# Feed-forward products in runs: all of a weight unit's 512-column products, then all of its 256-column ones

## The chip, the cores and the metric

The kernel runs on one core of one Trainium2 chip. The metric is the device time of one execution in microseconds. A profile of one execution gives, for each instruction, its engine, its source line, its start and its duration.

## What is computed

Two blocks of two layers each, on one sequence of 256 tokens with 1024 channels, all in float32. Each layer is a mixer and then a feed-forward stage with a residual. The mixers are a causal attention with rotary positions, a latent attention, a pooling mixer and an attention with a bias table. The four feed-forward stages have one form (2816 inner channels, a causal convolution of width 3 along the tokens, gelu in the first block and silu in the second):

```
g = xn @ w_gate
gc = conv_b + sum(conv_w[j] * shifted(g, 2 - j) for j in range(3))
h = act(gc) * (xn @ w_up)
x = x + h @ w_down
```

## The kernel before

**Splitting.** A float32 product is made of reduced-precision passes. A weight w is split into a high part `whi` and a low part `wlo = w - whi`; an activation x into `xx[:, k, 0, :]` (high) and `xx[:, k, 1, :]` (low). The products high*high, low(x)*high(w) and high(x)*low(w) are kept. Tokens are the columns that move through TensorE, 256 of them; the weight block of 128x128 is what is loaded before a product. With the high weight block loaded, both parts of x pass in one product of 512 columns (line 463); with the low weight block loaded, only the high part of x passes, 256 columns (line 465), added to the first 256 columns of the same PSUM bank. One 512 and one 256 product on one block are called a pair here. `block_wide` issues a pair; `across_wide` issues the pairs of the two output blocks m = 0 and 1 of one contraction block k, into the two banks of the PSUM tile it is given. So the order of TensorE was 512, 256, 512, 256, and so on, with a new weight block before every product. Where 512 columns are not used, `three` issues three products of equal width (lines 422 to 424).

**Weight units.** Weights come in units of up to 128x2048 elements, 180 in all, in the order of use. SyncE loads unit n into one of 3 `raw` buffers. ScalarE copies it, rounded, to one of 5 `whi` buffers (`hi(n)`, signalled by `s_hi`); VectorE subtracts to get `wlo` (`lo(n)`, signalled by `s_lo`, which also frees `raw`). TensorE waits on `s_lo` (`weights_here`) or `s_hi` (`high_here`), and its last product on a unit raises `s_used`, which frees the unit's ring place and tells ScalarE and VectorE that the bank is complete.

**A feed-forward stage** (`ffn(s)`, s is F0, F1, F2 or F3) has 34 units: eleven pairs of a gate unit and an up unit (each 8 k blocks by 2 output blocks), then twelve down units (four output groups c, each of 8, 8 and 6 k blocks over the 22 blocks of the hidden activation `hx`). The first gate and up units are interleaved block by block because the input blocks arrive one at a time. Gate and up results go to the PSUM tiles `banks0`, `banks1`, `TB` and `SB` in turn; `s_gr` and `s_ub` say that a tile has been read. ScalarE and VectorE make the convolution, the activation and the two parts of `hx` (`s_hl` counts finished blocks). For c = 0 TensorE waits on `s_hl` before each k, for c = 3 `last_pair` runs the block m = 0 in pairs and the block m = 1 with `three`.

**Other callers.** `across_wide` also serves `project`, the last two output units of each of the three attention mixers. Each engine runs its own list in a fixed order, written by hand; there is no planner.

In the profile, line numbers are those of the kernel file. Lines 679, 680 and 686 are products of 512 columns in the attention mixers (`high` and `low` in `heads_mixer`), where activations are the loaded block and weights move. Lines 518 and 519 are the two products that spread the sums of squares.

Of the kernel before, what the change touches and what calls it, by code (L numbers as in the profile page):

```python
# [14 lines left out]
S, D, KD = 256, 1024, 8  # L15
NF = 22
# [24 lines left out]
A, F0, B, F1, POOL, F2, DD, F3 = range(8)  # L41
# [59 lines left out]
def build(nc, dram, out):  # L101
    plan, first = unit_plan()
    N_UNITS = len(plan)
    with ExitStack() as ctx:
        def sb(name, shape, dt=F32, stack=ctx):
            return stack.enter_context(nc.sbuf_tensor(name, shape, dt))
# [5 lines left out]
        def sem(name):  # L112
            return ctx.enter_context(nc.semaphore(name))
# [8 lines left out]
        s_hi, s_lo, s_used = sem("s_hi"), sem("s_lo"), sem("s_used")  # L122
# [14 lines left out]
        s_act, s_hb, s_hh, s_hl = sem("s_act"), sem("s_hb"), sem("s_hh"), sem("s_hl")  # L137
# [22 lines left out]
        xx = sb("xx", [128, KD, 2, S], F32R)  # L160
# [15 lines left out]
        hx = sb("hx", [128, NF, 2, S], F32R, ffn_mem)  # L176
# [69 lines left out]
        def ffn_banks(s, i):  # L246

            b0, b1 = two_banks[FLIP[s]], two_banks[1 - FLIP[s]]  # L250
            return (TB, b0, b1, SB)[i % 4] if s == F2 else (b0, b1, TB, SB)[i % 4]
# [6 lines left out]
        def unit(n):  # L258
            _, _, nk, w = plan[n]
            r = n % RING  # L260
            return (whi[r][:, 0:nk * w].rearrange("p (k n) -> p k n", k=nk),
                    wlo[r][:, 0:nk * w].rearrange("p (k n) -> p k n", k=nk))
# [36 lines left out]
        def n_res(s, c):  # L299

            return 4 * s + c + 1
# [11 lines left out]
        def n_ff(s, i):  # L313

            return 11 * LAYER[s] + i + 1
# [104 lines left out]
        def tensor_program(e):  # L420
# [5 lines left out]
            def weights_here(n):  # L426
                e.wait_ge(s_lo, n + 1)

            def high_here(n):
                e.wait_ge(s_hi, n + 1)  # L430
# [13 lines left out]
            def x_here(s, k):  # L444
                e.wait_ge(s_xh, n_x(s, k))
                e.wait_ge(s_xl, n_x(s, k))
# [11 lines left out]
            def block_wide(n, po, m, k, a, kk, start, stop):  # L458


                wh, wl = unit(n)
                sl = slice(m * 128, (m + 1) * 128)
                e.matmul(po[:, 0:512], wh[:, k, sl], a[:, kk, :, :].rearrange("p w s -> p (w s)"), start=start,  # L463
                         stop=stop, skip_group_check=True)
                return e.matmul(po[:, 0:256], wl[:, k, sl], a[:, kk, 0, :], start=False, stop=stop,  # L465
                                skip_group_check=True)

            def across_wide(n, b, k, a, kk, start, stop):
                block_wide(n, b[:, 0, :], 0, k, a, kk, start, stop)
                return block_wide(n, b[:, 1, :], 1, k, a, kk, start, stop)  # L470

            def last_pair(s):


                b = ffn_banks(s, 5)
                for m in range(2):
                    kk = 0
                    for n, nk in zip(range(first[s] + 31, first[s] + 34), (8, 8, 6)):
                        wh, wl = unit(n)
                        if m == 0:  # L480
                            weights_here(n)
                        for k in range(nk):
                            start, stop = kk == 0, kk == NF - 1
                            if m == 0:
                                last = block_wide(n, b[:, 0, :], 0, k, hx, kk, start, stop)
                            else:
                                last = three(b[:, 1, 0:256], wh[:, k, 128:256], wl[:, k, 128:256], hx[:, kk, 0, :],
                                             hx[:, kk, 1, :], start, stop)
                            kk += 1
                        if m == 1:  # L490
                            last.then_inc(s_used, 1)
                    if m == 0:
                        last.then_inc(s_half, 1)
# [20 lines left out]
            def spread_sums(s):  # L514

                e.wait_ge(s_ones_r, 1)
                e.wait_ge(s_hs, LAYER[s] + 1)
                e.matmul(SB[:, 0, 0:256], ones_r[:, :], sx[:, 0, :], start=True, stop=False, skip_group_check=True)
                e.matmul(SB[:, 0, 0:256], ones_r[:, :], sx[:, 1, :], start=False, stop=True,
                         skip_group_check=True).then_inc(s_sum, 1)  # L520
# [7 lines left out]
            def ffn(s):  # L528
                u = first[s]
                bg, bu = ffn_banks(s, 0), ffn_banks(s, 1)  # L530
                weights_here(u + 1)
                if s != F2:
                    e.wait_ge(s_res, n_res(s - 1, 1))
                if s == F2:
                    for k in (0, 1):
                        x_here(s, k)
                        across_wide(u, bg, k, xx, k, k == 0, False)
                    e.wait_ge(s_uu, 2)
                    for k in (0, 1):
                        across_wide(u + 1, bu, k, xx, k, k == 0, False)  # L540
                for k in range(2 if s == F2 else 0, KD):
                    x_here(s, k)
                    last = across_wide(u, bg, k, xx, k, k == 0, k == KD - 1)
                    if k == KD - 1:
                        last.then_inc(s_used, 1)
                    last = across_wide(u + 1, bu, k, xx, k, k == 0, k == KD - 1)
                    if k == KD - 1:
                        last.then_inc(s_used, 1)
                if s != F2:
                    spread_sums(s)  # L550
                for i in range(1, 11):
                    n = u + 2 * i
                    bg, bu = ffn_banks(s, 2 * i), ffn_banks(s, 2 * i + 1)
                    weights_here(n)
                    if i >= 2:
                        e.wait_ge(s_gr, n_ff(s, i - 2))
                    for k in range(KD):
                        last = across_wide(n, bg, k, xx, k, k == 0, k == KD - 1)
                        if s == F2 and i == 1 and k == 0:
                            spread_sums(s)  # L560
                    last.then_inc(s_used, 1)
                    weights_here(n + 1)
                    if i >= 2:
                        e.wait_ge(s_ub, n_ff(s, i - 2))
                    else:
                        e.wait_ge(s_sr, LAYER[s] + 1)
                    for k in range(KD):
                        last = across_wide(n + 1, bu, k, xx, k, k == 0, k == KD - 1)
                    last.then_inc(s_used, 1)
                n = u + 22  # L570
                for c in range(4):
                    b = ffn_banks(s, 2 + c)
                    e.wait_ge((s_gr, s_ub)[c % 2], n_ff(s, 9 + c // 2))
                    if c == 3:
                        last_pair(s)
                        break
                    k0 = 0
                    for j, nk in enumerate((8, 8, 6)):
                        weights_here(n)
                        for k in range(nk):  # L580
                            if c == 0:
                                e.wait_ge(s_hl, n_ff(s, (k0 + k) // 2))
                            last = across_wide(n, b, k, hx, k0 + k, k0 + k == 0, k0 + k == NF - 1)
                        last.then_inc(s_used, 1)
                        n += 1
                        k0 += nk

# [556 lines left out]

            heads_mixer(A)
            ffn(F0)
            latent_mixer()
            ffn(F1)
            pool_mixer()
            ffn(F2)  # L1150
            heads_mixer(DD)
            ffn(F3)
# [1201 lines left out]
        @block.tensor  # L2354
        def _(e):
            tensor_program(e)
# [116 lines left out]
```

## Time and profile before

| | |
|---|---|
| median of 3 runs | 1072.65 us |
| lowest, highest | 1072.24, 1073.18 us |
| span of the profiled execution, first to last instruction | 1070.4 us |
| TensorE busy in it | 1064.7 us |
| VectorE, ScalarE busy in it | 839.0, 655.2 us |
| granted TensorE clock | full in all 40 slices |

The profile gives its execution's span and not a device time beside it: no time of its own for that execution is recorded apart from the three runs, whose median is 2.25 us above the span. A row of the chronological view gives the start of an instruction, its duration (for TensorE the modelled time to the end of the result, longer than the spacing of products, which overlap), the engine, the line, output<-moving operand, loaded operand, and the shapes. The spacing of products is read from the starts.

### The profile page before, as it was taken

The numbers are of one execution on the slowest core, as the hardware profiler recorded it, in microseconds if no ns is written. First come the engines' busy times: TensorE is split into PE (matmuls) and PEld (weight loads), VectorE is DVE, ScalarE is ACT, GpSimd is POOL, SyncE is SP. The second block draws the span as 40 slices with busy tenths as digits, with TensorE's granted clock in tenths as the row PEclk, the third lists the DMA queues.
The fourth block names the chain that finished last, engine by engine and source line by source line (L and its number), as shares of the span: only waits on it lengthen the run. The fifth ranks groups of instructions, "written<-read, shape, count | busy, mean of one in ns | idle before, by whom it ended". The sixth has DMA issues, their size and how long they took to land.

```text
span 1070.4 us, 16292 instructions
## 1 busy us (share of the span) xinstructions
PE 1064.7 (99%) x6536; PEld 932.3 (87%) x6536; DVE 839.0 (78%) x1364; ACT 655.2 (61%) x922; POOL 1.3 (0%) x8
## 2 busy tenths in 40 slices
PE   9999999999999999999999999999999999999998
PEld 7778888888898888888889888888877788888888
DVE  7985799886668779987667999876668768997852
ACT  7666567665458766765556577654456765776540
POOL 0000000000000000000000000000000000000000
PEclk9999999999999999999999999999999999999999
DMA  9552446555426155655552466455555533665540
GB/s 339 181 180 114 156 164 233 195 186 216 163 83 252 55 180 190 230 202 181 214 195 81 151 215 229 182 217 187 187 177 182 174 106 140 236 220 190 206 142 30
DMA packets 32091, 191.67 MB, mean 179 GB/s; under 512 B 4496, under 2 KB 6160, under 8 KB 12176
## 3 DMA queue, kind: packets, MB, share of 16 engines
q1 hardware_dynamic: 32016, 190.62, 50.3%
q8 instruction: 52, 0.85, 0.3%
q14 instruction: 23, 0.19, 0.1%
HBM read 189.56 MB, written 1.05 MB: 178 GB/s over the span
## 4 chain that ended last, share of the span: by engine, by line
PE 94%; DVE 2%; ACT 2%; issue 1%; DMA 0%; SPq 0%; DVEq 0%; ACTq 0%
PE banks L463 21%; PE TB L463 12%; PE SB L463 11%; PE banks L465 11%; PE TB L465 6%; PE SB L465 6%; PE banks L679 4%; PE banks L686 4%; PE banks L680 4%; PE banks L422 3%; PE banks L424 3%; PE banks L423 3%; PE banks L636 2%; PE TB L610 2%; PE SB L597 1%
## 5 line engine op out<-in xcount | busy, mean ns | idle before, releaser
L1712 DVE TENSOR_TENSOR wlo<-raw,whi 128x2048 fp32r<-128x2048 f32 (+2 forms) x180 | 395.8, 2201 | 78.6 <-ACT whi L1173 78.5
L1173 ACT ACTIVATE whi<-raw 128x2048 fp32r<-128x2048 f32 (+2 forms) x180 | 330.5, 1840 | 81.3 <-PE TB L465 25.6
L463 PE MATMUL banks<-xx,whi 128*128 128x512 f32 x752 | 262.2, 390 | 0.2 <-DVE wlo L1712 0.2
L465 PE MATMUL banks<-xx,wlo 128*128 128x256 f32 x752 | 212.1, 282 | 0.0
L463 PEld LDWEIGHTS banks<-xx,whi 128*128 128x128 f32 x752 | 141.2, 188 | 30.0 <-DVE wlo L1712 0.5
L465 PEld LDWEIGHTS banks<-xx,wlo 128*128 128x128 f32 x752 | 142.1, 189 | 0.0
L463 PE MATMUL TB<-xx,whi 128*128 128x512 f32 x336 | 117.8, 390 | 0.2 <-DVE xx L1717 0.2
L463 PE MATMUL SB<-xx,whi 128*128 128x512 f32 x320 | 111.8, 390 | 0.0
L465 PE MATMUL TB<-xx,wlo 128*128 128x256 f32 x336 | 94.7, 282 | 0.0
L463 PE MATMUL banks<-hx,whi 128*128 128x512 f32 x264 | 91.7, 390 | 0.0
L465 PE MATMUL SB<-xx,wlo 128*128 128x256 f32 x320 | 90.2, 282 | 0.0
L1258 ACT ACTIVATE ct<-gp,vec 128x256 f32<-128x256 f32 x88 | 48.2, 595 | 63.1 <-DVE gp L1879 63.1
L679 PE MATMUL banks<-whi,xx 128*128 128x512 f32 x192 | 78.0, 406 | 0.5 <-ACT whi L1665 0.5
L680 PE MATMUL banks<-whi,xx 128*128 128x512 f32 x192 | 75.9, 395 | 0.0
L463 PEld LDWEIGHTS TB<-xx,whi 128*128 128x128 f32 x336 | 63.1, 188 | 13.5 <-issue 0.3
L465 PE MATMUL banks<-hx,wlo 128*128 128x256 f32 x264 | 74.4, 282 | 0.0
L463 PEld LDWEIGHTS SB<-xx,whi 128*128 128x128 f32 x320 | 60.1, 188 | 12.6
L465 PEld LDWEIGHTS TB<-xx,wlo 128*128 128x128 f32 x336 | 63.5, 189 | 0.0
L463 PE MATMUL TB<-hx,whi 128*128 128x512 f32 x176 | 61.2, 390 | 0.0
L463 PE MATMUL SB<-hx,whi 128*128 128x512 f32 x176 | 61.2, 390 | 0.0
L465 PEld LDWEIGHTS SB<-xx,wlo 128*128 128x128 f32 x320 | 60.5, 189 | 0.0
L463 PEld LDWEIGHTS banks<-hx,whi 128*128 128x128 f32 x264 | 49.6, 188 | 10.4
(244 smaller groups left out, 1944.6 us busy)
## 6 DMA issues: line engine op xcount, KB each, us to landing
raw<-in_gate SPq DMA_DIRECT2D x44, 1024.0 KB, 4.7
raw<-in_up SPq DMA_DIRECT2D x44, 1024.0 KB, 4.8
raw<-in_down SPq DMA_DIRECT2D x32, 1024.0 KB, 4.8
raw<-in_down SPq DMA_DIRECT2D x16, 768.0 KB, 4.2
raw<-in_d_kq SPq DMA_DIRECT2D x8, 1024.0 KB, 5.0
raw<-in_a_kq SPq DMA_DIRECT2D x6, 1024.0 KB, 5.8
raw<-in_a_o SPq DMA_DIRECT2D x4, 1024.0 KB, 4.8
raw<-in_b_o SPq DMA_DIRECT2D x4, 1024.0 KB, 5.6
```

What stands on the lines that cost most here:

```text
L422: e.matmul(po, ah, bh, start=start, stop=False, skip_group_check=True)
L423: e.matmul(po, ah, bl, start=False, stop=False, skip_group_check=True)
L424: return e.matmul(po, al, bh, start=False, stop=stop, skip_group_check=True)
L463: e.matmul(po[:, 0:512], wh[:, k, sl], a[:, kk, :, :].rearrange("p w s -> p (w s)"), start=start, stop=stop, skip_group_check=True)
L465: return e.matmul(po[:, 0:256], wl[:, k, sl], a[:, kk, 0, :], start=False, stop=stop, skip_group_check=True)
L610: last = e.transpose(TB[:, a, c * 128:(c + 1) * 128], sc[:, a, c * 128:(c + 1) * 128], ident)
L679: e.matmul(po, xx[:, k, 0, sl], wh[:, k % 4, :], start=k == 0, stop=False, skip_group_check=True)
L680: e.matmul(po, xx[:, k, 1, sl], wh[:, k % 4, :], start=False, stop=False, skip_group_check=True)
L686: return e.matmul(slot_bank(s, i, h)[:, :], xx[:, k, 0, sl], wl[:, k % 4, :], start=False, stop=k == KD - 1, skip_group_check=True)
L1173: e.activation(whi[n % RING][:, 0:nk * w], raw[n % RAW][:, 0:nk * w], ACT.Copy).then_inc(s_hi, 1)
L1258: e.activation(ct[:, m, :], g[:, m, 0:S], ACT.Identity, scale=cw(0, 2 * i + m), bias=cb(2 * i + m)).then_inc(s_tap, 1)
L1712: e.tensor_tensor(wlo[n % RING][:, 0:nk * w], raw[n % RAW][:, 0:nk * w], whi[n % RING][:, 0:nk * w].bitcast(F32), ALU.subtract).then_inc(s ...
```

## The change

The products of a feed-forward unit are put in another order. A new function `whole_unit` waits for the unit's high part, issues its 512-column products for all k and both m, then waits for the low part and issues the 256-column ones for all k and both m. It serves the gate and up units from the second pair on, except the second gate unit of stage F2, and the down units of c = 0, 1, 2. `across_wide` keeps its callers (the first gate and up units, that one gate unit of F2, and `project`) but now issues 512, 512, 256, 256 for one k. `last_pair` is as it was. For c = 0 the waits on `s_hl` stand before the 512-column products of their k. The number, size and operands of the products are the same, and so are all signals.

```diff
--- before.py
+++ after.py
@@ -465,9 +465,42 @@
                 return e.matmul(po[:, 0:256], wl[:, k, sl], a[:, kk, 0, :], start=False, stop=stop,
                                 skip_group_check=True)
 
+            def wide_high(n, b, m, k, a, kk, start, stop):
+
+                wh, _ = unit(n)
+                return e.matmul(b[:, m, :], wh[:, k, m * 128:(m + 1) * 128],
+                                a[:, kk, :, :].rearrange("p w s -> p (w s)"), start=start, stop=stop,
+                                skip_group_check=True)
+
+            def wide_low(n, b, m, k, a, kk, stop):
+
+                _, wl = unit(n)
+                return e.matmul(b[:, m, 0:256], wl[:, k, m * 128:(m + 1) * 128], a[:, kk, 0, :], start=False,
+                                stop=stop, skip_group_check=True)
+
             def across_wide(n, b, k, a, kk, start, stop):
-                block_wide(n, b[:, 0, :], 0, k, a, kk, start, stop)
-                return block_wide(n, b[:, 1, :], 1, k, a, kk, start, stop)
+
+
+                for m in range(2):
+                    wide_high(n, b, m, k, a, kk, start, stop)
+                for m in range(2):
+                    last = wide_low(n, b, m, k, a, kk, stop)
+                return last
+
+            def whole_unit(n, b, nk, a, k0, count, done=None):
+
+
+                high_here(n)
+                for k in range(nk):
+                    if done is not None:
+                        e.wait_ge(s_hl, done(k))
+                    for m in range(2):
+                        wide_high(n, b, m, k, a, k0 + k, k0 + k == 0, k0 + k == count - 1)
+                weights_here(n)
+                for k in range(nk):
+                    for m in range(2):
+                        last = wide_low(n, b, m, k, a, k0 + k, k0 + k == count - 1)
+                last.then_inc(s_used, 1)
 
             def last_pair(s):
 
@@ -551,22 +584,22 @@
                 for i in range(1, 11):
                     n = u + 2 * i
                     bg, bu = ffn_banks(s, 2 * i), ffn_banks(s, 2 * i + 1)
-                    weights_here(n)
                     if i >= 2:
                         e.wait_ge(s_gr, n_ff(s, i - 2))
-                    for k in range(KD):
-                        last = across_wide(n, bg, k, xx, k, k == 0, k == KD - 1)
-                        if s == F2 and i == 1 and k == 0:
-                            spread_sums(s)
-                    last.then_inc(s_used, 1)
-                    weights_here(n + 1)
+                    if s == F2 and i == 1:
+                        weights_here(n)
+                        for k in range(KD):
+                            last = across_wide(n, bg, k, xx, k, k == 0, k == KD - 1)
+                            if k == 0:
+                                spread_sums(s)
+                        last.then_inc(s_used, 1)
+                    else:
+                        whole_unit(n, bg, KD, xx, 0, KD)
                     if i >= 2:
                         e.wait_ge(s_ub, n_ff(s, i - 2))
                     else:
                         e.wait_ge(s_sr, LAYER[s] + 1)
-                    for k in range(KD):
-                        last = across_wide(n + 1, bu, k, xx, k, k == 0, k == KD - 1)
-                    last.then_inc(s_used, 1)
+                    whole_unit(n + 1, bu, KD, xx, 0, KD)
                 n = u + 22
                 for c in range(4):
                     b = ffn_banks(s, 2 + c)
@@ -576,12 +609,7 @@
                         break
                     k0 = 0
                     for j, nk in enumerate((8, 8, 6)):
-                        weights_here(n)
-                        for k in range(nk):
-                            if c == 0:
-                                e.wait_ge(s_hl, n_ff(s, (k0 + k) // 2))
-                            last = across_wide(n, b, k, hx, k0 + k, k0 + k == 0, k0 + k == NF - 1)
-                        last.then_inc(s_used, 1)
+                        whole_unit(n, b, nk, hx, k0, NF, (lambda k: n_ff(s, (k0 + k) // 2)) if c == 0 else None)
                         n += 1
                         k0 += nk
```

## Rows read from the trace of the kernel before

**Rows 1.** The page: busy time, share of the span, instructions; granted clock in 40 slices.

```profile
PE 1064.7 (99%) x6536; PEld 932.3 (87%) x6536; DVE 839.0 (78%) x1364; ACT 655.2 (61%) x922; POOL 1.3 (0%) x8
...
PEclk9999999999999999999999999999999999999999
```

**Rows 2.** The page: the chain that ended last, share of the span by engine.

```profile
PE 94%; DVE 2%; ACT 2%; issue 1%; DMA 0%; SPq 0%; DVEq 0%; ACTq 0%
```

**Rows 3.** Waits of TensorE: line, releaser; us in total, times, longest.

```profile
PE SB L670 <- DVE ones L2297: 1.1, 1, 1.1
PE banks L679 <- ACT whi L1665: 0.5, 1, 0.5
PE banks L636 <- ACT pt L1307: 0.4, 1, 0.4
PE banks L463 <- DVE wlo L1712: 0.2, 1, 0.2
PE TB L463 <- DVE xx L1717: 0.2, 1, 0.2
```

**Rows 4.** Groups of TensorE products: count | busy us, mean ns of one | idle before.

```profile
L463 PE MATMUL banks<-xx,whi 128*128 128x512 f32 x752 | 262.2, 390 | 0.2 <-DVE wlo L1712 0.2
L465 PE MATMUL banks<-xx,wlo 128*128 128x256 f32 x752 | 212.1, 282 | 0.0
L463 PE MATMUL TB<-xx,whi 128*128 128x512 f32 x336 | 117.8, 390 | 0.2 <-DVE xx L1717 0.2
L463 PE MATMUL SB<-xx,whi 128*128 128x512 f32 x320 | 111.8, 390 | 0.0
...
L680 PE MATMUL banks<-whi,xx 128*128 128x512 f32 x192 | 75.9, 395 | 0.0
...
L424 PE MATMUL banks<-hx,wlo 128*128 128x256 f32 x88 | 24.5, 279 | 0.0
```

**Rows 5.** Chronological view, TensorE: pairs of stage F0, 320 from first to last row.

```profile
131.48 0.39 PE L463 MATMUL TB<-xx,whi 128*128 128x512 f32 x1
131.71 0.28 PE L465 MATMUL TB<-xx,wlo 128*128 128x256 f32 x1
...
242.42 0.39 PE L463 MATMUL TB<-hx,whi 128*128 128x512 f32 x1
```

**Rows 6.** The same view: 512-column products in a row, attention mixer, 30 between the rows.

```profile
11.48 0.40 PE L679 MATMUL banks<-whi,xx 128*128 128x512 f32 x1
11.71 0.40 PE L680 MATMUL banks<-whi,xx 128*128 128x512 f32 x1
...
18.48 0.40 PE L679 MATMUL banks<-whi,xx 128*128 128x512 f32 x1
```

**Rows 7.** The same view: 256-column products in a row, `last_pair`, 65 between the rows.

```profile
295.81 0.28 PE L422 MATMUL banks<-hx,whi 128*128 128x256 f32 x1
295.93 0.28 PE L423 MATMUL banks<-hx,whi 128*128 128x256 f32 x1
...
303.39 0.28 PE L424 MATMUL banks<-hx,wlo 128*128 128x256 f32 x1
```

**Rows 8.** The same view: first pairs after a stretch of 256-column products.

```profile
109.04 0.39 PE L463 MATMUL SB<-ox,whi 128*128 128x512 f32 x1
...
110.09 0.39 PE L463 MATMUL SB<-ox,whi 128*128 128x512 f32 x1
```

**Rows 9.** The same view, VectorE: last `hx` low part of F0, and a 512-column product of unit 3.

```profile
248.87 0.68 DVE L1863 TENSOR_TENSOR hx<-hb,hx 128x512 fp32r<-128x512 f32 x1
...
256.29 0.39 PE L463 MATMUL TB<-hx,whi 128*128 128x512 f32 x1
```

**Rows 10.** The same view: products (PE) and weight loads (PEld) in a stretch of pairs.

```profile
200.13 0.39 PE L463 MATMUL TB<-xx,whi 128*128 128x512 f32 x1
200.36 0.28 PE L465 MATMUL TB<-xx,wlo 128*128 128x256 f32 x1
...
200.13 0.19 PEld L465 LDWEIGHTS TB<-xx,wlo 128*128 128x128 f32 x1
200.36 0.19 PEld L463 LDWEIGHTS TB<-xx,whi 128*128 128x128 f32 x1
200.48 0.19 PEld L465 LDWEIGHTS TB<-xx,wlo 128*128 128x128 f32 x1
```

## The prediction

> **What bounds the kernel now.** I read the page first. TensorE is busy 99% of the span, and its granted clock is full in every slice [rows 1]. A busy TensorE is not yet a bound, since its products overlap, so the chain of work that ended last comes next: 94% of the span lies on TensorE, 2% each on VectorE and ScalarE, none on a transfer [rows 2]. The view of waits shows how little the engine stands still: the five waits listed for its products sum to 2.4 us, and only two of them, 0.2 us each, lie before a product that this change touches [rows 3]. So neither a weight part, nor an activation, nor a bank is late. The time is the sum of the spacings of 6536 products, and anything that changes a spacing goes into the end one to one.
>
> The groups say which products: line 463 with 512 columns and line 465 with 256, in equal number [rows 4]. The change concerns the order of these. By the code there are 4 stages x (352 gate and up + 132 down + 22 in the last group) = 2024 pairs, and 96 in the three mixers, 2120 in all.
>
> **The spacing of a pair.** Durations of products overlap, so I take starts. In stage F0 there are 20 units of 16 pairs from 131.48 to 242.42: 110.94 / 320 = 0.3467 us a pair, unit borders and waits included [rows 5]. Inside it the 512 takes 0.23 by its starts [rows 5]; the next paragraphs make it 0.2283, which leaves 0.1183 for the 256.
>
> **What a run of equal products costs.** The trace of before has no two 512-column products of line 463 in succession, but it has such runs elsewhere. Attention mixer: 30 products of 512 columns with a new loaded block each, 18.48 - 11.48 = 7.00 us, 0.2333 each [rows 6]. Last down group: 65 spacings of 256 columns, also with a new block each, 303.39 - 295.81 = 7.58 us, 0.1166 each; I use 0.1167 [rows 7]. Hence a 512 and a 256, each in its own run, cost 0.2333 + 0.1167 = 0.3500 us, against 0.3467 alternating: 0.0033 us more. The group durations have the same two shifts: 390 ns alternating against 395 in a run for 512 columns, 282 against 279 for 256 [rows 4]. Since the modelled duration moves with the spacing, the alternating 512 is 0.2333 - 0.005 = 0.2283, and the 256 is the rest of 0.3467, 0.1183.
>
> So alternation is what makes the present order cheap, and the trace shows it once more at another place. When pairs begin after a stretch of 256-column products, the first three take 110.09 - 109.04 = 1.05 us, 0.350 each, and only then the spacing settles at 0.3467 [rows 8]. The sizes are the same there; the neighbours before them are not. I can name no mechanism from this trace. Each weight load starts together with the product before its own, at 200.13 for the product of 200.36, and lasts 0.19 by its row [rows 10]; beside a 512 it has room, beside a 256 it has hardly any. The order 512, 256 pairs each load with a neighbour of the other size, which a run does not.
>
> **The change part by part.**
>
> 1. Units through `whole_unit`. Gate and up: 3 stages x 20 + 19 in F2 = 79 units x 16 pairs = 1264. Down, c = 0 to 2: 4 stages x (6 x 16 + 3 x 12) = 528. Together 1792 pairs, in runs of 16 or 12 products of a size. 1792 x 0.0033 = +6.0 us. The bounds: by the rows rounded to a hundredth, single 512-column spacings in the mixer reach 0.24; 0.235 with an unchanged 0.1183 would give 0.3533, +0.0067 x 1792 = +11.9 us. The lowest is a 512 that keeps 0.2283 in its run with a 256 at 0.1167: 0.3450, -0.0017 x 1792 = -3.0 us. I take the value in the middle because both its terms are measured in long runs of the same shape and type. What differs in the rows is the moving operand of the 512: weights there, activations here. For 256 columns the moving operand is the same `hx` that the down units use.
>
> 2. `across_wide` in the order 512, 512, 256, 256. It still serves 4 x 32 pairs of first units, 16 in F2 and 96 in the mixers, 240. Half of the neighbours are equal, so between 0 and 0.0033 a pair, 0 to +0.8 us; I take +0.4.
>
> 3. Changes of size. 115 units have one from 512 to 256 and one back. If a change gives back the advantage of one pair, that is 115 x 0.0033 = -0.4 us; after a stretch of 256s the rows show no advantage [rows 8]. Between 0 and -0.4, I take -0.2.
>
> 4. The wait on the high part, added at each unit's head. Behind it on TensorE stands everything else, but the wait it replaces was the later one (the low part is computed from the high part), and even that one ended at once but for one 0.2 us case in the gate unit of F2 that keeps its old form [rows 3]. 0 us. If the low parts were ever late, the new order would cover 16 x 0.2333 = 3.7 us of it; nothing is late, so this cover has nothing to hide and gains 0.
>
> 5. The waits on `s_hl` in c = 0. They now stand before the 512s only and so come earlier. The tightest is that for blocks 20 and 21, in the third down unit. Their low part is written until 248.87 + 0.68 = 249.55, and TensorE reached block 20 at 256.29 [rows 9]. In the new order two units of 16 x 0.350 = 5.6 us and eight 512s at 0.2333 go before it: 242.42 + 11.2 + 1.9 = 255.5. That leaves 5.9 us. 0 us. If it were gone, a stage could stop for what is missing, four times.
>
> 6. The end of a unit. The last product is a 256 as before and `s_used` comes with it, so the ring of 5 places and the banks are freed once per unit as before, 0.05 us later. ScalarE and VectorE have slack at that point: 61% and 78% busy [rows 1]. No transfer is moved, added or removed. 0 us.
>
> Sum: 6.0 + 0.4 - 0.2 = +6.2 us. Against the profiled execution: span 1070.4 to 1076.6 us. The median lies 2.25 us above that span, and I keep the difference: 1072.65 + 6.2 = 1078.85, given as 1078.8.
>
> A rule of the Trainium skill speaks against this. Its page "TensorE: Matmul & The Clock Gate", section "Back-to-back issue gap", gives the isolated spacing at the full clock as columns / 2.4 plus 2.5 ns, so 215.8 and 109.2 ns here, 325 ns a pair in any order; by that rule the sum would be 0. The same section says that in a real stream both the load and the product set the spacing. The trace differs from the formula in size, 346.7 ns a pair, and its rows show a dependence on the neighbours.
>
> **The rivals.**
>
> A. *The order does not matter.* A 512 keeps 0.2283 and a 256 keeps 0.1183 whatever stands next to them: 0.3467 a pair, 0 us, 1072.65. For it: a 512 has 390 ns in three different PSUM tiles, so the rhythm of a pair is very stable [rows 4]. Against it: 279 ns for the 256 in runs, and the first pairs of rows 8. The skill's formula named above is of this kind.
>
> B. *Faster: a run of 512s keeps the short spacing.* Place: the 512-column runs in 115 units. If the 0.2333 of the mixer belongs to moving weights and not to the run, the 512 stays at 0.2283, while the 256 drops to 0.1167 as in rows 7: -3.0 us, 1069.7. The point from which it decides is a 512 spacing of 0.3467 - 0.1167 = 0.2300; below that the kernel becomes faster. For it: only the moving operand distinguishes rows 6 from the new runs. Against it: the 256 spacing is about the same in the trace whichever operand moves, and the first pairs of rows 8 have long 512s with moving activations.
>
> C. *Slower by more.* The new runs cost more than those of the mixer, up to the upper bound of part 1, or an edge of a run costs something: 115 x 2 edges at 0.02 us would be +4.6. Together 1083 to 1085. For it: nothing direct. Against it: units border on one another without a gap now [rows 5].
>
> D. *The change does nothing to the waits either way*, which I take as part of the forecast: what it offers is cover for a late low part, and there is no late low part.
>
> **How the numbers follow.** Forecast (+5 to +8 us) 0.67; A 0.15; B 0.09; C 0.05; something between A and the forecast, +0.5 to +5 us, 0.04. The likeliest gives 1078.8, with 1077.5 to 1080.5 as its own range. The range with eight in ten has to reach down to A, as both bounds of the unknown 512 spacing count: 1072.2 to 1081.0 leaves out B and C. About 0.2%, 2.1 us, is what a measurement of this kernel can tell from no change. Faster by more than that: B, 0.09. Within: A and a little of the between, 0.17. Slower: the rest, 0.74.
>
> **What would show it.** In the changed profile the chronological view of a gate unit should have 16 rows of 512 columns with starts 0.233 apart and durations of 395 ns, then 16 of 256 columns at 0.117 and 279 ns; a unit should take 5.60 us in place of 5.55, and stages F0, F1 and F3 each some 1.5 us longer, the mixers nearly unchanged. The waits of TensorE should stay at about the same few tenths, without a new one on `hx`. The granted clock should stay full. The prediction is wrong if the 512 spacing in the run lies at or under 0.230, if a size change has a price of its own, or if waits on `whi` or `hx` appear.

## The result and the profile after

The changed kernel takes 1078.57 us, median of 4 runs (1078.29 to 1079.31), against 1072.53 us for the kernel before (4 runs): +6.0 us, ratio 1.0057 with an interval of 1.0044 to 1.0069. It is slower, near the 1078.8 us forecast.

The page of the changed kernel: busy time by engine, the granted clock, and the chain that ended last.

```profile
span 1077.5 us, 16292 instructions
...
PE 1071.0 (99%) x6536; PEld 926.2 (86%) x6536; DVE 839.5 (78%) x1364; ACT 655.2 (61%) x922; POOL 1.3 (0%) x8
...
PEclk9999999999999999999999999999999999999999
...
PE 94%; DVE 2%; ACT 2%; issue 1%; DMA 1%; SPq 0%; DVEq 0%; ACTq 0%
```

Nothing moved off or onto another engine against [rows 1, 2]: VectorE and ScalarE have the same work, the clock is full, and the whole difference is TensorE's. Its waits:

```profile
PE banks L707 <- ACT whi L1693: 1.3, 2, 0.8
PE SB L698 <- DVE ones L2325: 1.1, 1, 1.1
PE banks L664 <- ACT pt L1335: 0.4, 1, 0.4
PE banks L471 <- DVE wlo L1740: 0.2, 1, 0.2
PE TB L471 <- DVE xx L1745: 0.2, 1, 0.2
```

The feed-forward products (now lines 471 and 478) have the same two waits of 0.2 us as in [rows 3], and none on `hx`. The first row, at the weights of an attention mixer, is 0.8 us longer than before; this is part of why the span is 7.1 us longer and the median only 6.0. In every execution with both figures on record the device time lies 1.8 us above the span. By that the profiled execution of before, span 1070.4, took about 1072.2, its lowest time, while that of the changed kernel was the slowest of its four (1079.31).

The groups of TensorE: mean duration behind the comma.

```profile
L471 PE MATMUL banks<-xx,whi 128*128 128x512 f32 x752 | 191.9, 395 | 0.2 <-DVE wlo L1740 0.2
L478 PE MATMUL banks<-xx,wlo 128*128 128x256 f32 x752 | 104.6, 279 | 0.0
...
L471 PE MATMUL SB<-hx,whi 128*128 128x512 f32 x176 | 43.0, 395 | 0.0
```

390 and 282 ns became 395 and 279 [rows 4]. Busy time of a group is no measure here: 262.2 us fell to 191.9 because equal products now stand next to each other and their records overlap within the group, while the kernel got slower. The chronological view of stage F0 shows the spacing; equal neighbours are merged into one row with their count.

```profile
129.18 0.62 PE L471 MATMUL banks<-xx,whi 128*128 128x512 f32 x2
129.64 0.40 PE L478 MATMUL banks<-xx,wlo 128*128 128x256 f32 x2
129.88 0.62 PE L471 MATMUL banks<-xx,whi 128*128 128x512 f32 x2
...
132.19 3.90 PE L471 MATMUL TB<-xx,whi 128*128 128x512 f32 x16
135.92 2.03 PE L478 MATMUL TB<-xx,wlo 128*128 128x256 f32 x16
137.78 0.86 PE L471 MATMUL SB<-xx,whi 128*128 128x512 f32 x3
```

A unit in long runs takes 137.78 - 132.19 = 5.59 us (5.60 by the nanoseconds of the starts) in place of 16 x 0.3467 = 5.55: 3.73 / 16 = 0.233 for a 512 and 1.86 / 16 = 0.1165 for a 256. In the first units, where `across_wide` issues 512, 512, 256, 256, four products take 129.88 - 129.18 = 0.70, which the rows cannot tell from either value; the starts in nanoseconds give 0.6933, that is 0.3467 a pair, and nothing is lost.

### The profile page after: what moved, and what is told of

It reads as the page before. It is cut to its first block, busy times and chain, and to the rows that moved or that the text cites. A ratio compares the mean times of both kernels' runs of the same rounds, so it can differ in the third digit from the quotient of the medians.

```text
span 1077.5 us, 16292 instructions
## 1 busy us (share of the span) xinstructions
PE 1071.0 (99%) x6536; PEld 926.2 (86%) x6536; DVE 839.5 (78%) x1364; ACT 655.2 (61%) x922; POOL 1.3 (0%) x8
## 4 chain that ended last, share of the span: by engine, by line
PE 94%; DVE 2%; ACT 2%; issue 1%; DMA 1%; SPq 0%; DVEq 0%; ACTq 0%
PE banks L471 20%; PE TB L471 12%; PE SB L471 12%; PE banks L478 10%; PE TB L478 6%; PE SB L478 6%; PE banks L707 4%; PE banks L714 4%; PE banks L708 4%; PE banks L422 3%; PE banks L424 3%; PE banks L423 3%; PE banks L664 2%; PE TB L638 2%; PE banks L463 1%; PE SB L625 1%
## 5 line engine op out<-in xcount | busy, mean ns | idle before, releaser
L471 PE MATMUL banks<-xx,whi 128*128 128x512 f32 x752 | 191.9, 395 | 0.2 <-DVE wlo L1740 0.2
L471 PEld LDWEIGHTS banks<-xx,whi 128*128 128x128 f32 x752 | 133.8, 188 | 25.5 <-DVE wlo L1740 0.4
L478 PEld LDWEIGHTS banks<-xx,wlo 128*128 128x128 f32 x752 | 102.4, 188 | 9.0
L478 PE MATMUL banks<-xx,wlo 128*128 128x256 f32 x752 | 104.6, 279 | 0.0
L471 PE MATMUL TB<-xx,whi 128*128 128x512 f32 x336 | 82.9, 395 | 0.2 <-DVE xx L1745 0.2
L471 PEld LDWEIGHTS TB<-xx,whi 128*128 128x128 f32 x336 | 61.0, 188 | 13.2 <-issue 0.3
L714 PE MATMUL banks<-wlo,xx 128*128 128x512 f32 x192 | 55.2, 395 | 0.0
L1326 ACT ACTIVATE sc<-sc,small 128x128 f32<-128x128 f32 x96 | 42.4, 444 | 20.1 <-DVE small L1967 20.1
L707 PEld LDWEIGHTS banks<-whi,xx 128*128 128x128 f32 x192 | 36.1, 188 | 11.3 <-issue 2.2
L478 PE MATMUL TB<-xx,wlo 128*128 128x256 f32 x336 | 43.8, 279 | 0.0
L714 PEld LDWEIGHTS banks<-wlo,xx 128*128 128x128 f32 x192 | 36.1, 188 | 8.7
L471 PE MATMUL banks<-hx,whi 128*128 128x512 f32 x176 | 43.0, 395 | 0.0
```

Of the source, the lines that this page charges most:

```text
L471: return e.matmul(b[:, m, :], wh[:, k, m * 128:(m + 1) * 128], a[:, kk, :, :].rearrange("p w s -> p (w s)"), start=start, stop=stop, skip_ ...
L478: return e.matmul(b[:, m, 0:256], wl[:, k, m * 128:(m + 1) * 128], a[:, kk, 0, :], start=False, stop=stop, skip_group_check=True)
L707: e.matmul(po, xx[:, k, 0, sl], wh[:, k % 4, :], start=k == 0, stop=False, skip_group_check=True)
L714: return e.matmul(slot_bank(s, i, h)[:, :], xx[:, k, 0, sl], wl[:, k % 4, :], start=False, stop=k == KD - 1, skip_group_check=True)
L1326: last = e.activation(sc[:, a, sl], sc[:, a, sl], ACT.Exp, scale=-1.0, bias=low[:, 2 * h + a:2 * h + a + 1], accum_out=lsum[:, 2 * h + a:2 ...
```

## The experiments

**Runs of 2, 4, 8 and 3.** The changed kernel, with `whole_unit` changing the size after every G products, which is after G/2 blocks k. G is the length of a run, 2, 4 or 8; the kernels have the numbers 1, 2 and 4 where G // 2 stands here, and the one with runs of 3 goes through the (k, m) in threes.

```diff
-                for k in range(nk):            # all 512s, then all 256s
+                for g in range(0, nk, G // 2):
+                    ks = range(g, min(g + G // 2, nk))
+                    for k in ks:               # 512s of these k
...
+                    if g == 0:
+                        weights_here(n)
+                    for k in ks:               # 256s of these k
```

> Every unit that went through whole_unit issues two 512-column products, then two 256-column ones, for each k (runs of 2). The first units of each stage of the changed kernel already have this order, and their starts give 0.347 us a pair. Theory of the mix (two sizes in quick turn cost 13/12 of the columns' time, long runs of one size 35/32): 0.3467 us a pair, the time of the kernel before, 1072.5 us within 0.5. Theory of strict alternation (only a neighbour of the other size on both sides gives the short spacing): 0.350 a pair, as the changed kernel, 1078.6. Theory of the waits (the added waits cost the time): 1078.6 too, since they are all kept.

Measured: 1072.65 us, ratio 0.9998 (0.999 to 1.0007).

> Runs of 4: four 512-column products (two k), then four 256-column ones. Theory of edges (a product is short when one of its neighbours has the other size): half of the products are at an edge, 0.3483 us a pair, +3.0 us, 1075.5. Theory of the mix with a short memory: as runs of 2, 0.3467, 1072.5. Theory that a run of one size falls into its own rhythm at once: 0.350, 1078.6.

Measured: 1078.73 us, ratio 1.0053 (1.0040 to 1.0065).

> Runs of 8. Theory of edges: a quarter of the products at an edge, 0.3492 us a pair, +4.5 us, 1077. Theory of the mix: a gain that fades with the length of a run, between the run of 4 and the changed kernel. Theory that a run falls into its own rhythm at once: 0.350, 1078.6.

Measured: 1078.32 us, ratio 1.0050 (1.0038 to 1.0063).

> Runs of 3: three 512-column products, then three 256-column ones, and so on through a unit. Runs of 2 cost 0.3467 us a pair and runs of 4 cost 0.3500. If a product is short whenever it borders on the other size, two thirds of them do: about 0.348, 1074.6. If only a steady pattern of four products has the short rhythm: 0.350, 1078.5. If the limit lies between 3 and 4: 0.3467, 1072.5.

Measured: 1078.31 us, ratio 1.0054 (1.0040 to 1.0068).

It is a step, not a slope: runs of 2 cost nothing, runs of 3, 4, 8 and 16 cost the whole 6 us. The length of a stage, from the start of its first product to that of its last, shows it without the first mixer's waits, which vary between executions: F0 takes 183.25 us in the kernel before and 183.24 with runs of 2, but 184.74 in the changed kernel and with runs of 3, 4 and 8. Chronological view with runs of 2, where four products take (140.76 - 137.99) / 4 = 0.6925 us, or 0.346 a pair:

```profile
137.99 0.62 PE L471 MATMUL SB<-xx,whi 128*128 128x512 f32 x2
138.45 0.40 PE L478 MATMUL SB<-xx,wlo 128*128 128x256 f32 x2
...
140.76 0.62 PE L471 MATMUL SB<-xx,whi 128*128 128x512 f32 x2
```

and with runs of 4, where eight products take 1.40 us, 0.350 a pair:

```profile
138.51 1.09 PE L471 MATMUL SB<-xx,whi 128*128 128x512 f32 x4
139.45 0.63 PE L478 MATMUL SB<-xx,wlo 128*128 128x256 f32 x4
139.91 1.09 PE L471 MATMUL SB<-xx,whi 128*128 128x512 f32 x4
```

The theory of edges falls (it gave 1075.5 for 4 and 1077 for 8), and so does strict alternation (it gave 1078.6 for 2). Of the three readings set out for runs of 3, the one that came true is that only the steady pattern of four products, two of each size, has the short rhythm. With runs of 2 the kernel has every added wait of the change and the time of before, so the waits are free.

**One wait a unit.**

```diff
             def whole_unit(n, b, nk, a, k0, count, done=None):
-                high_here(n)
+                weights_here(n)
...
-                weights_here(n)
```

> The changed kernel with one wait a unit, on the low part, at its head, as the kernel before had it; the order of the products stays as changed. If the order of the products costs the time: 1078.6 within 0.5, ratio 1.0057. If the second wait in the middle of a unit costs it (115 units x 0.05 us): 1072.5.

Measured: 1078.31 us, ratio 1.0051 (1.0037 to 1.0065). The waits cost nothing from this side either; the order costs it.

**Bank and moving operand.** The output block m is the outer loop.

```diff
-                for k in range(nk):
-                    for m in range(2):
+                for m in range(2):
+                    for k in range(nk):
                         wide_high(...)
```

> The changed kernel with the output block m as the outer loop of both runs: the moving operand changes at every product and eight products in a row add to one PSUM bank; in the changed kernel two products in a row share the moving operand and the bank changes at every product. If bank or moving operand set the spacing, the 512-column products leave 0.2333 us (up or down by some ns). If only the sizes do: 0.2333 and 0.1167, a unit of 5.60 us, 1078.6.

Measured in one execution: 1078.27 us, beside 1072.40 for the kernel before. The spacings in its trace are those of the changed kernel, and F0 takes 184.74 us again. Neither the change of bank nor the shared moving operand matters.

**Zeros as weights.** The high part is made zero from the fourth unit on, so the 512-column products multiply by zeros; the low part is then the whole weight.

```diff
-                e.activation(whi[...], raw[...], ACT.Copy).then_inc(s_hi, 1)
+                e.activation(whi[...], raw[...], ACT.Copy, scale=0.0).then_inc(s_hi, 1)
```

> Changes the computation: the high part of each weight unit from the fourth on is made zero (the low part is then the whole weight), so the 512-column products multiply by zeros. Order and number of products as in the changed kernel. If the surplus over columns / 2.4 GHz comes from a limit on current, which depends on the data, the 512-column spacing falls from 233 toward 216 ns and the time by up to 30 us. If it is in the passing of operands: 233 ns, 1078.6 us.

Measured: 1078.47 us, one execution.

> Changes the computation in the same way, with the order of the kernel before. Limit on current: the pair falls below 0.3467 us. Passing of operands: 0.3467, 1072.5 us, and the difference of 6 us to its partner with the changed order stays.

Measured: 1073.33 us; the kernel before on the same chip took 1072.40. One execution too; it has 0.4 us more of waiting for `whi` in the first mixer. The spacings are unchanged in both (F0 takes 184.74 and 183.25 us), so the difference between the orders is not a matter of the values of these weights.

**Other widths.** Units 1 to 10 of each stage leave out part of the columns; only the high products of the first k keep 512.

```diff
+            RUN = {1: (512, 256), 2: (480, 240), 3: (448, 224), ..., 10: (192, 96)}
+            ALT = {1: (512, 256), 2: (512, 128), 3: (512, 384), ..., 10: (320, 320)}
+            # gate units: 16 products of RUN[i][0] columns, 16 of RUN[i][1]; up units: ALT[i] in turn
```

> Leaves out part of the computation: gate and up products of units 1 to 10 have fewer columns. Gate units are runs of 16 products, of 512, 480, 448, 416, 384, 352, 320, 288, 256 and 192 columns with the high part and of half as many with the low part; up units alternate two widths: 512 with 256, 128, 384, then 384 with 256, 384 with 384, 448 with 320, 480 with 240, 256 with 256, 512 with 512, 320 with 320. If a run costs 35/32 of the columns' time at 2.4 GHz at every width: 448 columns 204 ns, 320 columns 146 ns. The kernel before has a run of 384 at 173.4 (13/12), which speaks against that. If the surplus belongs to the two widths 512 and 256 (a step in the spacing): other widths lie at 13/12 or less. If alternation as such helps, 512 with 384 is below the mean of their runs; if only certain sums do, 320 with 320 and 384 with 384 are as in their runs.

One execution took 1036.45 us; the rhythm within each unit is what counts. Means of 12 spacings (for alternation, of 12 pairs) from the starts in F0. The surplus is what they exceed columns / 2.4 GHz by, the full granted clock:

| run of | spacing ns | surplus | | alternating | pair ns | surplus |
|---|---|---|---|---|---|---|
| 512 | 233.3 | 20.0 | | 512, 256 | 346.7 | 26.7 |
| 480 | 217.8 | 17.8 | | 512, 384 | 403.8 | 30.4 |
| 448 | 206.8 | 20.1 | | 448, 320 | 346.7 | 26.7 |
| 416 | 193.3 | 20.0 | | 384, 256 | 291.5 | 24.8 |
| 384 | 176.3 | 16.3 | | 480, 240 | 331.7 | 31.7 |
| 352 | 159.9 | 13.2 | | 384, 384 | 352.9 | 32.9 |
| 320 | 146.7 | 13.3 | | 512, 128 | 340.0 | 73.3 |
| 288 | 133.8 | 13.8 | | 512, 512 | 466.7 | 40.0 |
| 256 | 116.7 | 10.0 | | 320, 320 | 293.3 | 26.7 |
| 192 | 111.8 | 31.8 | | 256, 256 | 235.5 | 22.2 |

Runs of 224 columns and fewer stay at about 112 ns a product, whatever the width (a run of 240 takes 112.9). That the load of the next block sets this floor is a reading; no run tests it. From 256 up, the surplus of a run is 10, about 13, or 16 to 20 ns, and not a fixed share: 35/32 fits 512 and 256 and misses 448 (207 ns, not 204). Alternating 512 and 256 has 26.7, against 20.0 + 10.0 in runs. No fixed proportion gives this table: 480 with 240 has the same proportion as 512 with 256 and 5 ns more surplus. But it answers what the expectation asked of alternation. Two equal widths from the two weight buffers in turn gain nothing: 512, 384 and 320 take what they take in runs, 256 takes 2 ns more. Two different widths in turn are shorter than the sum of their two runs, by 1.5 ns (384, 256) to 7 ns (448, 320), except 480 with 240, which is 1 ns longer. Rows of the pair 512, 128 in the chronological view:

```profile
148.01 0.22 PE L496 MATMUL banks<-xx,wlo 128*128 128x128 f32 x1
148.07 0.44 PE L496 MATMUL banks<-xx,whi 128*128 128x512 f32 x1
148.35 0.22 PE L496 MATMUL banks<-xx,wlo 128*128 128x128 f32 x1
148.41 0.44 PE L496 MATMUL banks<-xx,whi 128*128 128x512 f32 x1
```

The 128 takes 0.06 and the 512 behind it 0.28 in place of 0.23, 0.34 together.

**Place of the operands.** 32 bytes of unused memory in each partition in front of the ten buffers of split weights and 32 behind. `off_line` is the kernel's own helper; both kernels already call it once, further back, in front of `vec`.

```diff
+        off_line("loaded")
         whi = [sb(f"whi{i}", [128, UNIT], F32R) for i in range(RING)]
         wlo = [sb(f"wlo{i}", [128, UNIT], F32R) for i in range(RING)]
+        off_line("back")
         gx = sb("gx", [128, KD + KD * S])
```

> The changed kernel with 32 bytes of unused memory before the ten buffers of split weights and 32 behind them, so that the loaded blocks of the feed-forward stages begin 32 bytes further, and xx too is moved by 64 in all. If the surplus comes from where the loaded block and the moving operand lie to each other, the spacings 0.2333 and 0.1167 change by some ns, 2112 pairs of them, several us. If place does not matter: unchanged, 1078.5.

One execution: 1069.62 us, the shortest time here of a kernel that computes everything, span 1067.8. (The pairs are 2120 in all; the 2112 of the expectation is a slip.)

> The same displacement in the kernel before. Place matters: a pair leaves 0.3467. Place does not matter: 1072.5, and the 6 us to its partner stay.

One execution: 1084.73 us, span 1082.9; the kernel before, 15 runs on the same chip, 1072.26 to 1073.02.

This turns the case round. With the operands where they were, long runs cost 6.0 us; with the split weights 32 bytes and all that lies behind them 64 bytes further, long runs are 15.1 us faster than alternation (1084.73 - 1069.62), by one execution each. The order before, displaced:

```profile
137.94 0.40 PE L465 MATMUL SB<-xx,whi 128*128 128x512 f32 x1
138.17 0.28 PE L467 MATMUL SB<-xx,wlo 128*128 128x256 f32 x1
...
140.06 0.40 PE L465 MATMUL SB<-xx,whi 128*128 128x512 f32 x1
```

Six pairs in 2.12 us are 0.353 a pair in place of 0.3467. The changed order, displaced:

```profile
142.64 3.84 PE L473 MATMUL banks<-xx,whi 128*128 128x512 f32 x16
146.32 1.98 PE L480 MATMUL banks<-xx,wlo 128*128 128x256 f32 x16
148.13 3.82 PE L473 MATMUL banks<-xx,whi 128*128 128x512 f32 x16
151.79 2.05 PE L480 MATMUL banks<-xx,wlo 128*128 128x256 f32 x16
153.67 1.09 PE L473 MATMUL TB<-xx,whi 128*128 128x512 f32 x4
```

One unit takes 148.13 - 142.64 = 5.49 us, the next 5.54, against 5.60 undisplaced. They differ from each other with the same products and widths. The weight buffer does not make the difference: in F0 all ten whole gate units take 5.49 and all ten up units 5.54, while the buffers go round five places, so that each place has both. So place changes the rhythm; the two sizes alone do not fix it.

Place and order do not fix it either. The displaced kernel before runs the same 320 pairs of twenty whole gate and up units in F0 and in F3, with `xx` at the same addresses and the weights going four times round the same five buffers. The row that begins them and the row behind them, in each stage:

```profile
132.28 0.40 PE L465 MATMUL TB<-xx,whi 128*128 128x512 f32 x1
...
245.35 0.40 PE L465 MATMUL TB<-hx,whi 128*128 128x512 f32 x1
...
906.26 0.40 PE L465 MATMUL TB<-xx,whi 128*128 128x512 f32 x1
...
1017.91 0.39 PE L465 MATMUL TB<-hx,whi 128*128 128x512 f32 x1
```

That is 113.07 / 320 = 0.3533 us a pair in F0 and 111.65 / 320 = 0.3489 in F3, at full granted clock in both; F1 is like F0, and the steady pairs of F2 too. The PSUM tiles `banks0` and `banks1` are exchanged in F3, but the units in `TB` and `SB`, which are not, differ as much. In the changed order, displaced, the long and the short units change places in F3: there the gate units take 5.54 and the up units 5.49. So something else counts too; that it is carried over from the products before, as in [rows 8], fits, but no run tests it.

**The mix in the attention mixers.** The kernel before, with each low product of 512 columns split in two and the order 512, 512, 256, 256.

```diff
-                    return e.matmul(slot_bank(s, i, h)[:, :], xx[:, k, 0, sl], wl[:, k % 4, :], ...)
+                    for c in (slice(0, 256), slice(256, 512)):
+                        last = e.matmul(po[:, c], xx[:, k, 0, sl], wl[:, k % 4, c], ...)
...
-                    for k in range(4 * part, 4 * part + 4):
-                        high(i, h, k)
                     if h == 0:
                         weights_here(n)
                     for k in range(4 * part, 4 * part + 4):
+                        high(i, h, k)
                         last = low(i, h, k)
```

> The kernel before; in the two attention mixers each 512-column product with the low weight part is made two of 256 columns (a further weight load each), and the quarters issue 512, 512, 256, 256 for each k instead of eight 512s and then four 512s. If the mix of sizes has the short rhythm here too, with weights as the moving operand: 128 low products, three products of 0.2333 become four in 0.6933, -0.0067 us each, -0.85 us, ratio 0.9992, which the starts can show and the times hardly. If each further product costs a surplus of its own of 10 to 13 ns, the two 256s cost 0.2333 to 0.2367: 0 to +0.4 us. The first four slots that keep their order (both_halves) stay at 0.2333.

Measured: 1073.80 us, ratio 1.0011 (1.0002 to 1.0020): the wrong side of the first theory and above the +0.4 us of the second. In its chronological view four products take 0.702 us, (35.38 - 31.17) / 6, not 0.6933, beside 0.700 for the three that they replace:

```profile
30.40 0.47 PE L679 MATMUL banks<-whi,xx 128*128 128x512 f32 x1 [0.25 <-DVE wlo L1714]
...
31.17 0.39 PE L679 MATMUL banks<-whi,xx 128*128 128x512 f32 x1
31.40 0.40 PE L680 MATMUL banks<-whi,xx 128*128 128x512 f32 x1
31.63 0.40 PE L688 MATMUL banks<-wlo,xx 128*128 128x256 f32 x2
...
35.38 0.40 PE L679 MATMUL banks<-whi,xx 128*128 128x512 f32 x1
```

The short rhythm of 512, 512, 256, 256 does not carry over to the mixers, where the roles of weights and activations are exchanged and the operands lie elsewhere. The first row shows a second price: with the order 512, 512, 256, 256 the low part is needed at the head of a unit, and there TensorE now waits for it, 0.25 us. The spacing makes 128 x 0.0017, about 0.2 us, the wait 0.25; the rest of the 1.2 us has no cause shown.

## Why the prediction was right, point by point

*Bound.* Right: TensorE's spacings set the end and nothing else moved. One figure of the setting was off without effect: the offset from span to device time is 1.8 us and not 2.25, but the forecast adds its difference to the median and does not need it.

*Part 1, long runs, +6.0 us.* Right in sign and size. The spacings of line 471 and 478 are 0.233 and 0.1165 to 0.117 as read from [rows 6, 7], and four kernels (changed, runs of 8, one wait, m outermost) lie between 1078.3 and 1078.6 with these spacings. Stages F0 and F1 grow by 1.49 us each and F2 by 1.45, as the 1.5 a stage that was forecast; the mixers stay, but for the waits of the first. What made it right deserves a reserve: I carried the 0.2333 over from products whose operands lie elsewhere, and named only the moving operand's kind as a difference. The displaced kernels show that a change of place alone moves a pair from 0.3467 to 0.353 or 0.349 (alternating) and from 0.3500 to 0.343 or 0.346 (in runs). The rows of the mixer gave the value that this placement also gives; that they had to was not shown by any row, and that they did is in part luck. The reason offered beside the sum, that alternation puts a neighbour of the other size beside each product, does not hold: in runs of 2 only one neighbour differs and nothing is lost, in runs of 3 two thirds of the products border on the other size and everything is lost.

*Part 2, `across_wide`, +0.4 us.* Too much: 0.3467 a pair in the first units, the 32 pairs of `project` behind the first mixer take 10.98 us after 10.99 before, and the kernel with runs of 2 in every whole unit has the time of before. It measures 0. Half-equal neighbours do not mean half the loss.

*Part 3, changes of size, -0.2 us.* 0 within what can be read: a unit takes 5.60 us, which is 16 x 0.3500, with nothing given back.

*Parts 4 to 6, waits and release, 0.* Right: the one-wait kernel and the runs of 2 show it from both sides, and no wait on `hx` appears. The margin that was forecast for blocks 20 and 21, 5.9 us, is there: their low part is written until 251.31 and TensorE reaches them at 257.25. The two small mis-sized terms have opposite signs; the sum without them is +6.0, what was measured.

*Rivals.* A (order without effect) is refuted here, and the dependence on order is larger still after displacement. The Trainium skill, "TensorE: Matmul & The Clock Gate", section "Back-to-back issue gap", whose formula for an isolated product is of this kind, stands 17.5 ns under the trace for a 512 in a run (215.8 against 233.3), and that formula has no term for neighbours or place. B is refuted for the kernel as it is. With the displacement the 512s in a run fall to 3.66 / 16 = 0.229 and 3.68 / 16 = 0.230, at or just under the 0.2300 named as the point of decision, and that kernel's one execution is shorter than the kernel before; but the cause there is place, not B's, which was what moves. C did not occur.

*What stays open.* Why the spacing depends on run length with a step between 2 and 3, on width without a rule, on 32 and 64 bytes of displacement, and, after displacement, on the stage. It is shown that the values of the high weights, the bank, the waits and the order of m and k have no part in the 6 us, and that the place of the operands changes the spacing. That the read of the loaded block and that of the moving operand come into each other's way is a guess that no run tests, and a pattern set by place and order alone does not fit the two values in F0 and F3. The displacement moved the weights by 32 and everything behind them by 64 bytes, both at once; which of the two acts was not tried, nor whether the 1069.62 and 1084.73 us hold over several executions. The first is one execution, 2.6 us under the lowest of the 15 runs of the kernel before.

## What to carry to other kernels

When TensorE never waits, read the spacing of starts, not busy time or durations: it is the unit in which an order of products is paid, and 3 ns a pair were 6 us here. Alternating a wide and a narrow product or issuing them in runs is not good or bad in itself; the same edit cost 6 us in one placement of the buffers and, by one execution of each order, gained 15 us in another 32 to 64 bytes away. So measure an order together with a displacement of its operands, an edit of two lines, before either is judged.

## What was not expected of the hardware

Displacing memory by 32 and 64 bytes moved the alternating pairs by +7 ns in three stages and +2 ns in the fourth, and the pairs in runs by about -3.5 or -7 ns, mostly in turn from unit to unit, with the same instructions. Runs of 2 kept the short rhythm and runs of 3 lost all of it. A 128-column product between 512s made the pair 340 ns, only 6.7 less than with twice its columns, and runs of 224 columns and fewer did not get shorter than about 112 ns a product.
